# Two attentions of a float32 transformer kernel: the 16 meta keys of eight heads turned and multiplied at once, the value sums of eight heads kept in two banks

## What is computed

```python
N_META, BLOCK_Q = 16, 128
MLA_HEADS = FOX_HEADS = 16           # 64 value columns per head

def attend(qb, qpos, cq=None):
    s = jnp.einsum('bhqd,bhkd->bhqk', qb, k) * scale
    if cq is not None:
        s = s + (cq[..., :, None] - cum[:, :, None, :])
    s = jnp.where(key_pos[None, :] <= qpos[:, None], s, -jnp.inf)
    p = jax.nn.softmax(s, axis=-1)
    return jnp.einsum('bhqk,bhkd->bhqd', p, v)
...
y_mla = (o_mla * jax.nn.silu(z_mla)) @ w_br_mla
y_fox = (o_fox * jax.nn.silu(z_fox)) @ w_br_fox
mixed = (jax.nn.sigmoid(gate_a) * y_mla + jax.nn.sigmoid(gate_b) * y_fox) @ w_out
```

## Time and profile before

| | |
|---|---|
| median of 3 runs | 1001.35 us (1000.96 to 1002.16) |
| the profiled execution | 1001.34 us, span 999.5 us |
| PE busy | 957.9 us, 96% of the span |
| DVE, ACT busy | 592.5 us (59%), 482.3 us (48%) |
| DMA | 149 GB/s over the span |
| mean granted clock of PE | 0.994 |

### The profile page before, as it was taken

The page is one execution under the profiler, slowest core; times in us unless marked ns, Lnnn a source line. Parts: engine busy times, 40 slices in busy tenths (PEclk is TensorE's granted clock), DMA queues, the critical chain, the costliest instruction groups (busy, mean ns, idle before and its releaser), DMA issues.

```text
span 999.5 us, 14170 instructions
## 1 busy us (share of the span) xinstructions
PE 957.9 (96%) x5243; PEld 802.3 (80%) x5243; DVE 592.5 (59%) x1103; ACT 482.3 (48%) x768; POOL 22.6 (2%) x41
## 2 busy tenths in 40 slices
PE   6999799999999999999999999999999999999996
PEld 6877587888888899778888888879988887887875
DVE  4856657745455578556453635776554655665565
ACT  5545546535353447454443434675344444434542
POOL 0003100000000000000000000000000000000000
PEclk9999999999999999999999999999999999999998
DMA  6642245463645522246545464322233233333441
GB/s 215 237 169 85 84 184 180 161 230 148 224 153 198 181 85 86 85 150 224 212 150 228 145 233 173 123 106 107 92 120 127 85 127 127 133 120 127 153 163 43
DMA packets 25319, 149.25 MB, mean 149 GB/s; under 512 B 2992, under 2 KB 3120, under 8 KB 11056
## 3 DMA queue, kind: packets, MB, share of 16 engines
q1 hardware_dynamic: 24624, 146.39, 40.2%
q0 software_dynamic: 640, 2.11, 0.7%
HBM read 147.45 MB, written 1.05 MB: 149 GB/s over the span
## 4 chain that ended last, share of the span: by engine, by line
PE 73%; DVE 7%; ACT 5%; DVEq 3%; issue 2%; ACTq 0%
PE bank L435 21%; PE bank L436 21%; PE bank L437 21%; ACT w_hi L1184 2%; PE bank L506 1%; DVEq L2058 1%; DVE w_lo L1705 1%; PE bank L700 1%; DVE arena L2083 1%; PE bank L983 1%; PE bank L968 1%; PE bank L815 1%; PE bank L1004 1%; PE bank L1005 1%; PE bank L1003 1%
## 5 line engine op out<-in xcount | busy, mean ns | idle before, releaser
L435 PE MATMUL bank<-w_hi,x_hi 128*128 128x512 f32 (+2 forms) x648 | 262.7, 405 | 3.7 <-DVE ffn_nat L1955 1.4
L436 PE MATMUL bank<-w_lo,x_hi 128*128 128x512 f32 (+2 forms) x648 | 254.1, 392 | 0.0
L437 PE MATMUL bank<-w_hi,x_lo 128*128 128x512 f32 (+2 forms) x648 | 252.0, 389 | 0.0
L1619 DVE TENSOR_TENSOR w_lo<-w_raw,w_hi 128x2048 fp32r<-128x2048 f32 x52 | 118.8, 2292 | 62.2 <-ACT w_hi L1123 61.2
L435 PEld LDWEIGHTS bank<-w_hi,x_hi 128*128 128x128 f32 x648 | 122.3, 189 | 33.2 <-issue 5.8
L1705 DVE TENSOR_TENSOR w_lo<-w_raw,w_hi 128x2048 fp32r<-128x2048 f32 x50 | 114.4, 2290 | 51.3 <-ACT w_hi L1184 50.6
L437 PEld LDWEIGHTS bank<-w_hi,x_lo 128*128 128x128 f32 x648 | 121.7, 188 | 27.1
L436 PEld LDWEIGHTS bank<-w_lo,x_hi 128*128 128x128 f32 x648 | 122.0, 188 | 22.4
L1123 ACT ACTIVATE w_hi<-w_raw 128x2048 fp32r<-128x2048 f32 x54 | 103.1, 1916 | 58.4 <-DMA w_raw<-w_main_dram 51.5
L1184 ACT ACTIVATE w_hi<-w_raw 128x2048 fp32r<-128x2048 f32 x50 | 95.0, 1908 | 13.9 <-PE bank L437 9.6
L1323 ACT ACTIVATE ffn_nat<-bank,stat 128x256 f32<-128x256 f32 x44 | 20.8, 473 | 134.2 <-PE bank L437 134.1
(11 more groups left out here) (349 smaller groups left out, 1526.1 us busy)
## 6 DMA issues: line engine op xcount, KB each, us to landing
w_raw<-w_main_dram SPq DMA_DIRECT2D x111, 1024.0 KB, 4.9
s_raw<-w_side_dram SPq DMA_DIRECT2D x51, 512.0 KB, 4.2
h<-x_dram SPq DMA_DIRECT2D x2, 512.0 KB, 3.9
w_raw<-w_main_dram SPq DMA_DIRECT2D x2, 512.0 KB, 6.7
arena<-rows_dram POOLq DMA_DIRECT2D x2, 512.0 KB, 4.1
out_dram<-arena SPq DMA_DIRECT2D x1, 512.0 KB, 2.6
out_dram<-arena SPq DMA_DIRECT2D x2, 256.0 KB, 2.0
arena<-c_b_dram POOLq DMA_DIRECT2D x1, 264.0 KB, 2.8
```

The lines of the kernel that those rows point to most:

```text
L435: pe.matmul(out, ah, bh, start=first, stop=False)
L436: pe.matmul(out, ah, bl, start=False, stop=False)
L437: return pe.matmul(out, al, bh, start=False, stop=last)
L1619: dve.tensor_tensor(w_lo[:, slot, 4 * g:4 * g + 4, :], w_raw[:, g, :, :], w_hi[:, slot, 4 * g:4 * g + 4, :], ALU.subtract).then_inc(w_lo_o ...
```

## The change

Meta keys. ACT no longer copies a turned meta tile per head. After the exponentials of head n+1 it copies the 2 x 16 meta columns of head n out of `sm` into `meta_p` (`meta_kept`), eight heads side by side, 128 columns. Once per eight heads (in steps 8, 16, 24 and 31) PE turns the two tiles of `meta_p` (`meta_turn`), ACT copies them into `pt`, and PE multiplies them by a 128 x 512 block-diagonal matrix of the meta values of eight heads (`meta_values`). That matrix is made four times (steps 1, 2, 7 and 10): PE multiplies a matrix of repeated identities with the 16 rows of meta values (`spread`, result 128 x 512), and DVE multiplies the result by `own_block`, a mask of the blocks. `repeat` and `own_block` are made by DVE ahead of the heads. POOL's two zero fills go.

Value sums. The values of eight heads stand side by side in banks 6 (first query block) and 7 (second); `values` has three matmuls left and waits no longer for each head's output but once per group. DVE keeps the reciprocals per head (`head_root`) and takes all eight outputs in two products of 512 columns (`group_out`). `turn` has three transposes left.

Keys. The spreads and the turned tiles need a bank each: `after_rider(n)` puts ("um", c), ("fm", c) and ("mt", g) into the key list, behind the first rider key of their step. DVE's masking of head n waits in addition until the meta columns of head n-2 have been copied (`mp_ok`).

The diff, cut to its core:

```diff
@@ -90,6 +90,18 @@
 TAIL_KEYS = [("brf", c, r) for c in range(2) for r in range(R)]
+GROUP = 8
+SPREADS = {1: ("um", 0), 2: ("um", 1), 7: ("fm", 0), 10: ("fm", 1)}
+def after_rider(n):
+    extra = [SPREADS[n]] if n in SPREADS else []
+    if n and n % GROUP == 0 or n == 2 * NH - 1:
+        extra.append(("mt", n // GROUP if n == 2 * NH - 1 else n // GROUP - 1))
+    return extra
@@ -107,7 +119,7 @@
             keys.append(("uq", n + 3))
-        keys += RIDERS[n]
+        keys += RIDERS[n][0:1] + after_rider(n) + RIDERS[n][1:]
     keys += TAIL_KEYS + [("out", c, r) for c in range(2) for r in range(R)]
@@ -246,6 +258,10 @@
         q_h, sm, pt = ar(14720, 2, S), ar(15232, 2, 416), ar(16064, 640)
+        meta_p = [ar(off, R, GROUP * M) for off in (5760, 6016, 14720, 14976)]
+        repeat, own_block = ar(4736, P), ar(4864, GROUP)
+        meta_v = [v_mm[:, 0:CH], v_mm[:, CH:D], f_vm[:, 0:CH], f_vm[:, CH:D]]
+        root_p = stat[:, 8:24].rearrange("p (r a) -> p r a", r=R)
         b2c, b2k = ar(16704, L + S), ar(15232, L + P)
@@ -991,19 +1003,44 @@
                 pe.transpose(bank[5][:, P:2 * P], s_[:, 2 * M + P:2 * M + 2 * P], ident[:, :])
-                pe.transpose(bank[5][:, 2 * P:3 * P], s_[:, 2 * M + 2 * P:416], ident[:, :])
-                pe.transpose(bank[6][:, 0:P], s_[:, 0:P], ident[:, :])
-                pe.transpose(bank[6][:, P:2 * P], s_[:, M + P:M + 2 * P], ident[:, :]).then_inc(pt_ps, 1)
-
-            def values(n, v, vm):
-                pe.wait_ge(pt_ok, n + 1)
-                pe.wait_ge(ptm_ok, n - A2 + 1)
-                pe.wait_ge(o_ok, n)
-                pe.matmul(bank[7][:, 0:HD], pt[:, 384:384 + P], vm, start=True, stop=False)
-                pe.matmul(bank[7][:, 0:HD], pt[:, 0:P], v(0), start=False, stop=True)
-                pe.matmul(bank[7][:, HD:2 * HD], pt[:, 384 + P:640], vm, start=True, stop=False)
-                pe.matmul(bank[7][:, HD:2 * HD], pt[:, P:2 * P], v(0), start=False, stop=False)
-                pe.matmul(bank[7][:, HD:2 * HD], pt[:, 2 * P:3 * P], v(1), start=False, stop=True).then_inc(o_ps, 1)
+                pe.transpose(bank[5][:, 2 * P:3 * P], s_[:, 2 * M + 2 * P:416], ident[:, :]).then_inc(pt_ps, 1)
+            def values(n, v):
+                pe.wait_ge(pt_ok, A2 + n + 1)
+                first = n % GROUP == 0
+                if first and n:
+                    pe.wait_ge(og_ok, n // GROUP)
+                at = slice(n % GROUP * HD, (n % GROUP + 1) * HD)
+                pe.matmul(bank[6][:, at], pt[:, 0:P], v(0), start=first, stop=False)
+                pe.matmul(bank[7][:, at], pt[:, P:2 * P], v(0), start=first, stop=False)
+                pe.matmul(bank[7][:, at], pt[:, 2 * P:3 * P], v(1), start=False, stop=False)
+            def meta_turn(g):
+                b = acc_wait(("mt", g))
+                pe.wait_ge(mp_ok, GROUP * (g + 1))
+                for r in range(R):
+                    ins = pe.transpose(b[:, r * P:(r + 1) * P], meta_p[g][:, r, :], ident[:, :])
+                done(ins, ("mt", g))
+            def meta_values(g):
+                evacuated(("mt", g), (("um", "fm")[g // 2], g % 2))
+                for r in range(R):
+                    ins = pe.matmul(bank[6 + r][:, :], pt[:, 384 + r * P:384 + (r + 1) * P], meta_v[g], start=False, stop=True)
+                ins.then_inc(og_ps, 1)
+            def spread(key):
+                b = acc_wait(key)
+                if key[0] == "um":
+                    pe.wait_ge(rep_ok, 1)
+                    pe.wait_ge(vu_ok, key[1] + 1)
+                    src = v_mm
+                else:
+                    pe.wait_ge(vm_ok, key[1] + 1)
+                    src = f_vm
+                done(pe.matmul(b[:, :], repeat[0:M, :], src[0:M, key[1] * CH:(key[1] + 1) * CH], start=True, stop=True), key)
@@ -1071,9 +1106,18 @@
                 riders(RIDERS[n], 0)
+                last = n % GROUP == 0 and n // GROUP
+                if last:
+                    meta_turn(last - 1)
                 if n:
                     head_values(n - 1)
                 turn(A2 + n)
+                if n in SPREADS:
+                    spread(SPREADS[n])
+                if last:
+                    meta_values(last - 1)
+                if n == 2 * NH - 1:
+                    meta_turn(n // GROUP)
                 if n in MLA_TURNS:
@@ -1084,6 +1128,7 @@
             head_values(2 * NH - 1)
+            meta_values(2 * NH // GROUP - 1)
@@ -1492,8 +1537,10 @@
                 for cc in range(2):
+                    if (i, cc) == (1, 1):
+                        act.drain().then_inc(vu_ok, 2)
                     if t == 2:
-                        act.wait_ge(vz_ok, 2)
+                        act.wait_ge(tp_ready, ST["cqkv"] + ST_TILES["cqkv"])
                         carry(v_mm[0:M, cc * CH:(cc + 1) * CH], ("uv", i, cc), rows=M)
@@ -1560,10 +1606,15 @@
-            def meta_turned(n):
-                act.wait_ge(pt_ps, n + 1)
-                act.wait_ge(o_ps, n)
-                act.activation(pt[:, 384:640], bank[6][:, 0:2 * P], ACT.Copy).then_inc(ptm_ok, 1)
+            def meta_kept(n):
+                act.drain()
+                kept = sm[:, n % 2, 0:2 * (M + P)].rearrange("p (r x) -> p r x", r=R)[:, :, 0:M]
+                at = slice(n % GROUP * M, (n % GROUP + 1) * M)
+                act.activation(meta_p[n // GROUP][:, :, at], kept, ACT.Copy).then_inc(mp_ok, 1)
+            def meta_turned(g):
+                carry(pt[:, 384:640], ("mt", g), width=2 * P)
@@ -1576,7 +1627,9 @@
                     rider(keys[0])
-                meta_turned(A2 + n)
+                meta_kept(n)
+                if n and n % GROUP == 0 or n == 2 * NH - 1:
+                    meta_turned(after_rider(n)[-1][1])
                 if n in MLA_TURNS:
@@ -2208,6 +2261,10 @@
             dve.drain()
+            dve.tensor_copy(repeat[0:M, :].rearrange("p (a m) -> p a m", a=GROUP),
+                            ident[0:M, 0:M].rearrange("p (a m) -> p a m", a=1).to_broadcast([M, GROUP, M])).then_inc(rep_ok, 1)
+            dve.tensor_reduce(own_block, ident[:, :].rearrange("p (a m) -> p a m", m=M), mybir.AxisListType.X, ALU.add)
+            dve.drain()
             rest_half(C_FK + 1, (C_FK + 1) % 2, 1)
@@ -2271,14 +2328,38 @@
             def head_masked(n):
+                if n >= 2:
+                    dve.wait_ge(mp_ok, n - 1)
                 s_ = sm[:, n % 2, :]
                 b = sc_bank[n % 2]
                 masked(A2 + n, lambda r: s_[:, 0:M + P] if r == 0 else s_[:, M + P:416],
                        lambda r: b[:, 0:M + P] if r == 0 else b[:, M + P:416],
                        lambda r: c_mask[:, P:L] if r == 0 else c_mask)
-            def head_out(n):
-                attended(A2 + n, (o_mla if n < NH else o_fox)[:, :, n % NH * HD:(n % NH + 1) * HD])
+            def head_root(n):
+                s0 = 8 * (n % 4)
+                dve.wait_ge(p_ok, A2 + n + 1)
+                dve.reciprocal(root_p[:, :, n % GROUP], small[:, s0 + 4:s0 + 6])
+            def group_out(g):
+                dve.wait_ge(og_ps, g + 1)
+                dve.drain()
+                cols = slice(g % 2 * CH, (g % 2 + 1) * CH)
+                for r in range(R):
+                    ins = dve.tensor_tensor((o_mla if g < 2 else o_fox)[:, r, cols].rearrange("p (a e) -> p a e", a=GROUP),
+                                            bank[6 + r][:, :].rearrange("p (a e) -> p a e", a=GROUP),
+                                            root_p[:, r, :].rearrange("p (a e) -> p a e", e=1).to_broadcast([P, GROUP, HD]),
+                                            ALU.mult)
+                ins.then_inc(og_ok, 1)
+                dve.drain()
+            def spread(key):
+                dve.tensor_tensor((v_mm if key[0] == "um" else f_vm)[:, key[1] * CH:(key[1] + 1) * CH].rearrange("p (a e) -> p a e", a=GROUP),
+                                  acc_in(key)[:, :].rearrange("p (a e) -> p a e", a=GROUP),
+                                  own_block.rearrange("p (a e) -> p a e", e=1).to_broadcast([P, GROUP, HD]),
+                                  ALU.mult).then_inc(acc_free[USE[key] % 2], 1)
@@ -2299,9 +2380,13 @@
                 if n:
-                    head_out(n - 1)
+                    head_root(n - 1)
                 dve.wait_ge(pt_ps, A2 + n + 1)
                 dve.tensor_copy(pt[:, 0:384], bank[5][:, 0:384]).then_inc(pt_ok, 1)
+                if n in SPREADS:
+                    spread(SPREADS[n])
+                if n and n % GROUP == 0:
+                    group_out(n // GROUP - 1)
                 if n in MLA_TURNS:
...
```

More of the change, by code:

```diff
@@ L311, in two_blocks @@
             sem(n) for n in ("sc_ps", "nm_ok", "p_ok", "pt_ps", "pt_ok", "ptm_ok", "o_ps", "o_ok"))
-        k_ok, vz_ok, cum_ok = sem("k_ok"), sem("vz_ok"), sem("cum_ok")
+        k_ok, cum_ok = sem("k_ok"), sem("cum_ok")
         f_ps, f1_ok, f2_ok, ncum_ok, kpe_ps, kp_ok, kr_ps = (
@@ L316, in two_blocks @@
```

(17 more changed lines are left out.)

## The result

The changed kernel takes **1019.91 us** (median of 4 runs, 1018.57 to 1023.91), the kernel before 1001.55 us beside it: a ratio of **1.019, 95% interval 1.016 to 1.022**. I had forecast 1007.0 us, at most 1010.5. The direction is right, the size is three times as large.

A forecast was written before the change was run, and what follows sets the result against it. PE was taken as the bound: 11.2 us of work added less 21.1 removed is -9.9, plus 15.6 of waits makes 5.7 us more, 1001.34 to 1007.0 us. The range holding 8 in 10 was 1000.5 to 1010.5.

The forecast's parts named there:

- What bounds the kernel: In the middle of the heads PE is busy 59.37 of 60 us, so PE is the bound.
- work removed: Two value matmuls and two transposes fewer on PE per head: 0.66 us, for 32 heads 21.1 us.
- Waits: New PE waits for banks and copies, mainly at heads 1, 7, 8, 10, 16 and 24: 15.6 us in sum.
- The first query: At the start, DVE's copy, reduce and drain ahead of the split that this query waits for: 0.45 us more.
- The end of the program: The last meta product moves PE by 1.3 us; the later gatings add a wait of 0.4 us.
- The chain of head 16: PE's meta product waits 3.8 us for ACT's copy, behind head 17's exponentials, DVE's masking and a 2.29 us split.
- the riders of heads 17 and 25: Each stands on the bank of the rider before it, with the scores between: 0.2 us each, 0.4 in all.
- the clock falls in the wait of head 16: Rival: PE at half clock after that wait, costing 2.4 us: 1009.4 us, or 1011.8 if head 24 too; chance 0.13.
- Spreads: Four wide f32 matmuls on PE, priced by columns at 0.86 us each, like the eight meta products.
- Savings: 0.66 us less PE work at each of the 32 heads.
- The waits are covered: Rival at ACT's list: splits, masking and evacuations come earlier, some 3 us of waits stay; 994 us, chance 0.14.
- half of it: Rival: group waits hold, spreads and small terms come at half; waits of 8 to 12 us, 999.5 to 1003.3, chance 0.13.

The follow-up runs named there:

- x7_w1710: Kernel before, plus a wait on PE behind the turn of heads 1, 7 and 10 for DVE's copy of it: 1007.55 us, ratio 1.0067.
- x1_side_late: Changed kernel, with idle bank 2 for spreads and turned meta tiles and the group's product behind the rider's second half: 997.08 us, ratio 0.9958 to the kernel before.
- x10_w8to15: Kernel before, plus a wait on PE behind the turn of each head from 8 to 15 for DVE's copy of it: 1018.33 us, ratio 1.0175.
- x6_w1624: Kernel before, plus a wait on PE behind the turn of heads 16 and 24 for ACT's copy of it: 1008.42 us, ratio 1.0076.
- x9_w710b: Kernel before, plus a wait on PE behind the turn of heads 7 and 10 only for DVE's copy of it: 1007.75 us, ratio 1.0068.
- x8_rows128: As x1_side_late, but the spread multiplies 128 rows, 112 of them zeros, instead of 16: 996.92 us, ratio 0.9958 to the kernel before.

## Why the prediction was wrong, step by step

**What bounds the kernel, and work removed: right.** Most heads gain 0.66 to 0.73 us, as forecast.

**Waits: right, as idle time.** Forecast against measured, in us: head 7 1.6 and 1.55, head 8 1.8 and 1.56, head 10 1.6 and 1.89, head 16 3.8 and 3.67, head 24 2.9 and 2.84, head 1 0.8 and 0.74. The first query waits 1.36 where it waited 0.93, 0.43 more against 0.45. The end of the program grows by 1.6 against 1.7. The chain of head 16 is the one worked out: ACT's copy, at 832.93, stands right behind the exponentials and the copy of the meta columns (0.23 us). Only the riders of heads 17 and 25 (0.4) did not wait.

**The step that failed** is the rival "the clock falls in the wait of head 16", which I had priced at 2.4 us, confined to heads 16 and 24, and given 0.13, since the one fall in the earlier trace rows followed a wait of 4.77 us. I took that row as if it were a bound: shorter waits keep the clock. It was no bound, only the one wait that I looked at. The clock fell at five of six waits, of 0.74 to 3.67 us, and that cost 10.3 us in the profiled execution, nearly twice my whole forecast of 5.7. The trace of before could not have settled it: its longest wait within the heads kept the clock. Timeline of PE and windows view of the kernel before:

```profile
713.68 0.39 PE L435 MATMUL bank<-x_hi,w_hi 128*128 128x256 f32 x1 [1.50 <-DVE w_lo L1705]
...
680.00:760.00 80.00, 77.93 (x567) 70.92 (x566) 47.22 (x109) 36.01 (x63) 0.00 (x0) 1.00 0.32 114
```

This wait is in the profiles of all twelve kernels, at 1.50 to 1.52 us, and no fall follows it in any. So the trace of before gave a fall at 4.77 us and none at 1.50, and between the two, where five of my six forecast waits lay (1.6 to 3.8), nothing at all. The sixth, of 0.8, lay under both, and the clock fell behind it all the same.

The Trainium skill (TensorE: Matmul & The Clock Gate, "Why this matters for your kernels") advises against idle gaps between bursts that are longer than four of the five waits here after which the clock fell. In these runs shorter gaps were followed by a fall too: 1.32 us by itself (x7_w1710), 0.74 us with a spread behind it. The prediction applied that advice to heads 16 and 24 alone.

**Mis-sized terms.** Spreads: 4 x 0.86 forecast, 4 x 1.25 measured, +1.6 us. I priced by columns and took the rows of the stationary side to be free. The meta products did cost 0.86 each: in x1_side_late the step at head 8 takes 1.04 us more than before, and two products less the 0.66 saved are 1.06. Savings: 0.66 at every head forecast, nothing at heads 6, 14, 18 and 28, +2.7 us, +0.8 in parts at others. The earlier trace rows shows one such wait for `s_lo`, and I read it for the restart and not for what it means: where PE waits already, it cannot gain.

The sum for the profiled execution: 22.6 us of span (2.3 ahead of the values of head 0, 18.6 up to those of head 31, 1.6 behind), of which 5.7 forecast, 10.3 clock, 1.6 spreads, 3.5 savings not arrived, 1.9 more at the start than forecast (within what executions differ by there), less 0.4, which is what remains for the small terms. The median lies 18.4 us over before; those runs have less half clock (0.985 to 0.987 against 0.982).

**The other rivals.** "The waits are covered" and "half of it" did not come about: no wait was covered, and the spreads' waits came at their full size.

## What to carry to other kernels

On a kernel whose TensorE is busy throughout, price a new wait of about 1 us or more not at its length alone, but up to its length plus one fall of the clock, here 1.5 to 3.0 us each in the changed kernel and some 0.7 to 1.6 behind waits alone. Six waits of 0.74 to 3.67 us cost almost as much in clock (10.3 us) as in idle time (12.25 us). Before counting a saving on the bound engine, list the waits that it already has downstream: each of them takes the saving of one step. And a bank that stands idle, or a product that is moved behind other work, can turn the same change from 1.9% slower to 0.4% faster.

## What the runs showed of the hardware

The granted clock fell to half behind single waits of 1.32, 2.14, 2.23 and 2.94 us with nothing but the former work around them (x7_w1710, x10_w8to15, x6_w1624), and stayed full behind others of 0.88, 1.50, 1.79, 2.08 and 2.09. Next to the products of the change it fell behind 0.74, 1.55 and 1.89 us, each with a spread behind it, and stayed full behind 1.56 with two transposes behind it. By these profiles neither the length nor the place decides alone; that the same kernel does one or the other from execution to execution is inferred from the mean clocks of x9_w710b (0.994 in two, 0.990 in two). What else decides stays open. Neither what the engine did before the wait, nor what came right behind it, nor when the wait came was tried by itself; a spread of 128 rows behind a wait, or a spread moved away from its wait, would test the second.

A float32 matmul with 16 rows on the stationary side and 512 columns took 1.25 us among other work (x1_side_late), the same with 128 rows 0.86 (x8_rows128). The Trainium skill (TensorE: Matmul & The Clock Gate, "Why this matters for your kernels") says in its line on small K that one matmul of 32 rows takes as long as one of 128. The runs here have 16 rows and float32, and there it was slower.
